# Hybrid decoder step: the compressed-branch bias read back through DRAM, position weights as the streamed operand, one source for the norms' mean, and constant products on TensorE inside three norms

## The chip, the cores and the metric

The kernel runs on one core of one Trainium2 chip. The metric is the device time of one execution in microseconds. The engines are TensorE (PE, its weight load PEld), VectorE (DVE), ScalarE (ACT), GpSimd (POOL) and SyncE (SP); SP issues DMAs and waits on semaphores.

## What is computed

One step of a two-layer decoder on 512 prompt tokens and 8 sequences of 8 new tokens, 576 tokens in all, 1024 features. Layer 1 is a Mamba-2 mixer, layer 2 an attention with three branches (compressed, selected, window) that read one shared K/V projection. Each layer has two normed residuals.

```python
def layer_norm(x, g, b):
    mu = jnp.mean(xf, axis=-1, keepdims=True)
    var = jnp.mean(jnp.square(xf - mu), axis=-1, keepdims=True)
    return ((xf - mu) * lax.rsqrt(var + LN_EPS)).astype(x.dtype) * g + b
# per layer
h = layer_norm(DN_ALPHA * h + mix, ln_g[i, 0], ln_b[i, 0])
h = layer_norm(DN_ALPHA * h + sq_relu_mlp(h, mlp_w1[i], mlp_w2[i]), ln_g[i, 1], ln_b[i, 1])
# compressed keys and values: 32 tokens each, a position row pe added to every token
part = chunks[:, r:r + n_cmp] + pe[r * CMP_STRIDE:(r + 1) * CMP_STRIDE][:, None, :]
hid = hid + jnp.einsum('bcjgd,jde->bcge', part, w1[r])
# compressed scores: a bias by distance, from a table of 32 buckets x 16 heads
s_c = s_c + bias_hgr[rel_bucket(pos[:, None] - cmp_end[None, :])].transpose(0, 2, 3, 1)
```

## The kernel before

**Layout and order.** Activations lie by feature: `xT` is 128 partitions x 8 chunks x 576 tokens. Every engine has its own program, written out by hand; semaphores order them, and each engine runs its program in order.

**Dense products.** Weights come as slots of 128 x 1024 (512 KB). SP loads a slot into one of two places of `ring`; ScalarE rounds it to the high part, GpSimd subtracts to the low part, into one of two places of `split`. A place of `ring` is free when its slot is split, a place of `split` when TensorE has used it. `dense_block` (line 1245) runs 48 products a slot: 8 chunks, three pairs of high and low parts, two halves of 288 tokens. `stream` on SP (line 594) is the loop of loads.

**Norms.** `last_projection` (line 1294) makes the projection ahead of a norm, eight blocks. VectorE adds each block to `xT` as it comes (`last_residuals`, line 1945) and adds chunks up into `row`: chunks 0 to 6 go into it, chunk 7 is left to TensorE as a second source. `layer_norm(k)` on TensorE (line 1486), for k = 0 to 3: sums by token of `row` (`by_token`: six products of 96 tokens x one column, two passes each) and of `xT`'s last chunk into `s1`, of the squares into `s2`; then the mean spread over all partitions into `flat_x`, from both sources (lines 1496, 1497); then, after VectorE and ScalarE have made 1/sqrt of the variance (lines 1968 to 1979), the scale spread into `flat_s` (line 1501). VectorE subtracts and multiplies by chunk (lines 1982, 1985), ScalarE applies g and b twice (lines 1106, 1107), once rounded into `xs`, and GpSimd makes the low part. The next projection's first block takes the chunks as they come.

**Bias tables.** Inside the first MLP, `bias_tables` on TensorE (line 1504) makes the bias by distance for 16 heads, `bt` (1040 distances), and then for the compressed branch `cbt`: 56 products of 128 distances x 16 heads (line 1517), one for each shift by 16. SP stores `bt` to DRAM (`bscr`, line 611), copies its rows 128 times to `bskew` (line 615), loads the strips `Rs` from there (line 619) and copies 16 pieces of them into `nr` (line 624), with one pair of weight slots in between each time. These stand in SP's program among the loads for the second matrix of the first MLP half, `S_M2[0][0]`.

**Compression weights.** `cw1` (2 MB) holds the compression's first matrices. GpSimd issues its load (line 840) behind `mlp_los(0, 1, ...)`, that is behind the splits for the second norm's projection, since its place holds `ef`, `eb` and `bt` until then. The position rows times `cw1` are 32 products (`position_sums`, line 1540) with `cw1` held and one column streamed, five after each chunk of the K/V projection's first block; ScalarE copies the result to `hpe` (line 1110).

Of the kernel before, what the change touches and what calls it, by code (L numbers as in the profile page):

```python
# [85 lines left out]
def build(nc, a):  # L86

    with ExitStack() as ctx:
# [131 lines left out]
        at[0] = KC * T  # L220
        bd = carve(512)
# [54 lines left out]
        CEN, SQS = zip(*((v[:, 0, :], v[:, 1, :]) for v in (spare, spare_x, spare, spare_x)))  # L276
        ptab = sb("ptab", [1, NB * NPG], I32)
# [215 lines left out]
        s1 = dense[0:TQ, 0, 0:2 * TC].rearrange("p (c k) -> p c k", k=2)  # L493
# [96 lines left out]
        def _(sp):  # L590
# [3 lines left out]
            def stream(first, last):  # L594
                with sp.Fori(first // NSLOT, last // NSLOT) as i:
                    for j in range(NSLOT):
# [46 lines left out]
        def _(pool):  # L643
# [194 lines left out]
            pool.wait_ge(cbt_ready, 1)  # L838
# [78 lines left out]
        def _(act):  # L917
# [180 lines left out]
            def layer_norm(k):  # L1098

                act.wait_ge(ln_stats, 2 * k + 1)  # L1100
                act.activation(lnt[:, 2, :], lnt[:, 2, :], ACT.Sqrt, bias=eps[0:TQ, 0:1]).then_inc(ln_root, 1)
                for m in range(KC):
                    act.wait_ge(ln_scaled, k * KC + m + 1)
                    ends = dict(bias=lnb[:, k, m:m + 1], scale=lng[:, k, m:m + 1])
                    if k < 3:
                        act.activation(xs[:, 0, m, :], xT[:, m, :], ACT.Identity, **ends).then_inc(xh_ready, 1)
                    act.activation(xT[:, m, :], xT[:, m, :], ACT.Identity, **ends).then_inc(x_ready, 1)
                if k == 1:
                    act.wait_ge(pe_done, 1)
                    act.activation(hpe, dense[:, 3, 0:2], ACT.Copy).then_inc(hpe_ready, 1)  # L1110
# [133 lines left out]
        def _(pe):  # L1244
# [31 lines left out]
            def projection(b0, s0, blocks, nsl, hi, lo, ready=None, rounded=None, after=None):  # L1276

                for j in range(2):
                    dense_block(b0 + j, s0 + j * nsl, nsl, hi, lo, ready=ready if j == 0 else None,
                                rounded=rounded if j == 0 else None, after=after if j == 0 else None)  # L1280
                    if after and j == 0:
                        pe.wait_ge(hpe_ready, 1)
# [255 lines left out]
            pe.wait_ge(s_cw1, 16)  # L1538

            def position_sums(k):  # L1540


                for j in range(5 * k, min(5 * k + 5, 32)):
                    kv, i = divmod(j, 16)
                    mm = pe.matmul(dense[:, 3, kv:kv + 1], cw1[:, kv, i // 8, i % 8, :],
                                   cpe[:, kv, i // 8, i % 8:i % 8 + 1], start=i == 0, stop=i == 15)
                if k == KC - 2:
                    mm.then_inc(pe_done, 1)

            projection(B_KV, S_KV, SL_KV, 1, x_h, x_l, (x_split, 2 * KC), (xh_ready, KC), position_sums)
# [43 lines left out]
            def compressed(s_):  # L1596
                pe.wait_ge(hpe_ready, 1)
# [178 lines left out]
        def _(dve):  # L1776
# [168 lines left out]
            def last_residuals(k):  # L1945
# [13 lines left out]
                for m in range(2, KC):  # L1959
# [3 lines left out]
                    if m < KC - 1:  # L1963
                        dve.wait_ge(blk_evac, b0 + m + 1)
                        dve.wait_ge(ln_sum, 6 * k + m - 1)
                        dve.tensor_tensor(row[:, :], row[:, :], xT[:, m, :], ALU.add).then_inc(ln_sum, 1)

            def layer_norm(k):
                dve.wait_ge(ln_tok, 3 * k + 2)
                link(dve, "dve", dve.tensor_reduce(lnt[:, 0, :], s1, AX.X, ALU.add))  # L1970
                link(dve, "dve", dve.tensor_tensor(lnt[:, 1, :], lnt[:, 0, :], lnt[:, 0, :], ALU.mult))
                dve.wait_ge(ln_tok, 3 * k + 3)
                link(dve, "dve", dve.tensor_reduce(lnt[:, 0, :], s2, AX.X, ALU.add))
# [43 lines left out]
            flat = cbt.rearrange("p s h -> p (s h)")  # L2017
            dve.tensor_copy(flat[:, 0:512], bS[:, 0, :])
            dve.tensor_copy(flat[:, 512:NSIG * NH], bS[:, 1, 0:NSIG * NH - 512]).then_inc(cbt_ready, 1)
# [67 lines left out]
            def shift_compressed(qt):  # L2087
# [6 lines left out]
                dve.wait_ge(pcs_done, qt + 1)  # L2094
                s0 = 24 - 8 * qt
# [317 lines left out]
```

## Time and profile before

| | us |
|---|---|
| median of 3 runs | 2146.24 (2142.49 to 2151.03) |
| profiled execution, its own time | 2147.33 |
| its span | 2145.7 |
| granted TensorE clock, mean share of full | 0.937 |

The profile is one execution. Busy time is time in which an engine ran an instruction; a row of the timeline merges neighbours of one form and says what ended the idle time ahead of them. Windows give the granted clock of TensorE as a share: 1.00 is 2.4 GHz, 0.50 is 1.2 GHz. Products in fp32 run as two passes, each counted as an instruction. DMA issues on SP stand as SPq rows.

### The profile page before, as it was taken

The page shows a single profiled execution, that of the slowest core. Times are in us where ns is not written, and L with a number is a line of the kernel's source. Part 1 is how long each engine was busy: PE and PEld are TensorE (multiplying, and loading weights), DVE is VectorE, ACT ScalarE, POOL GpSimd, SP SyncE. Part 2 cuts the span into 40 slices and gives each one's busy share as a digit, 9 for nine tenths or more (in the row PEclk, how much of TensorE's full clock was granted, in tenths as well). Part 3 has the DMA queues.
Part 4 walks back from the last instruction along what each step waited for, and adds up shares of the span by engine and source line. Part 5 has one row for each costly group of instructions (what it writes and reads, how often), then busy time and mean ns, then how long its engine had stood idle before and what let it go on. Part 6 is the DMA issues. An engine that isn't in the chain of part 4 may idle for free.

```text
span 2145.7 us, 36763 instructions
## 1 busy us (share of the span) xinstructions
PE 1982.5 (92%) x14824; PEld 1817.4 (85%) x14824; DVE 866.9 (40%) x1712; ACT 652.0 (30%) x1115; POOL 973.5 (45%) x697
## 2 busy tenths in 40 slices
PE   7989898978979998999999998989978999999997
PEld 5988887857778998999998998955547899999996
DVE  7484766847455210012233112167745621002134
ACT  3443343432133211122223113166634422112222
POOL 2444445446437642356453333344412565345552
PEclk9999999978998988999996998989999899999998
DMA  4211213122131215322221243350060122222221
GB/s 167 71 50 64 104 40 119 50 81 92 50 114 60 81 67 127 100 79 80 87 79 69 79 152 116 87 204 1 21 236 25 56 79 86 81 79 88 79 79 64
DMA packets 52629, 184.61 MB, mean 86 GB/s; under 512 B 7070, under 2 KB 11838, under 8 KB 50976
## 3 DMA queue, kind: packets, MB, share of 16 engines
q1 hardware_dynamic: 40272, 129.66, 18.3%
q0 software_dynamic: 9952, 50.08, 6.5%
q10 hardware_dynamic: 2288, 3.23, 0.4%
q8 instruction: 84, 1.38, 0.3%
q14 instruction: 33, 0.27, 0.0%
HBM read 166.59 MB, written 27.28 MB: 90 GB/s over the span
## 4 chain that ended last, share of the span: by engine, by line
PE 68%; DVE 12%; issue 9%; POOL 5%; ACT 4%; DMA 1%; ACTq 0%; SPq 0%; POOLq 0%; DVEq 0%
PE dense L1269 48%; PE dense L1592 3%; POOL split L673 3%; DVE tile L1908 2%; PE dense L1675 2%; PE bS L1381 2%; DVE tile L1818 2%; PE dense L1632 1%; PE bXM L1662 1%; POOL tile L780 1%; POOL hid L805 1%; PE bXM L1443 1%; PE bXM L1388 1%; PE dense L1710 1%; DVE tile L1811 1%
## 5 line engine op out<-in xcount | busy, mean ns | idle before, releaser
L1269 PE MATMUL dense<-xs,split 128*128 128x288 f32 x6848 | 984.7, 302 | 32.3 <-DVE y_lo L1936 9.2
L1269 PEld LDWEIGHTS dense<-xs,split 128*128 128x128 f32 x6848 | 948.7, 193 | 64.5 <-issue 51.7
L673 POOL TENSOR_TENSOR split<-ring,split 128x1024 fp32r<-128x1024 f32 x212 | 533.6, 2517 | 846.6 <-ACT split L932 825.4
L932 ACT ACTIVATE split<-ring 128x1024 fp32r<-128x1024 f32 x212 | 224.6, 1059 | 830.5 <-PE dense L1269 816.1
L1269 PE MATMUL dense<-hid,split 128*128 128x288 f32 x3072 | 417.1, 298 | 6.0 <-POOL split L673 6.0
L1269 PEld LDWEIGHTS dense<-hid,split 128*128 128x128 f32 x3072 | 415.6, 191 | 6.3 <-POOL split L673 6.3
L1830 DVE SCALAR_TENSOR_TENSOR tile<-tile,dense 128x576 f32<-128x576 f32 (+1 forms) x56 | 42.2, 754 | 422.9 <-PE dense L1269 422.9
L1995 DVE TENSOR_SCALAR sq<-dense 128x576 f32<-128x576 f32 x64 | 48.5, 758 | 310.5 <-PE dense L1269 310.5
L903 POOL TENSOR_SCALAR tile<-tile,tile,tile 128x128 f32<-128x128 f32 (+3 forms) x128 | 78.3, 626 | 80.1 <-DVE tile L2159 80.1
L805 POOL TENSOR_TENSOR hid<-sq,hid 128x576 f32 x64 | 77.2, 1206 | 0.0
L1171 ACT ACTIVATE tile<-tile,tile 128x128 f32<-128x128 f32 (+3 forms) x128 | 70.5, 553 | 18.2 <-DVE tile L2144 18.0
L1818 DVE SCALAR_TENSOR_TENSOR tile<-tile,tile,tile 128x512 f32<-128x512 f32 x72 | 69.5, 966 | 2.6
L1592 PE MATMUL dense<-tile,tile 128*128 128x128 f32 x576 | 66.4, 274 | 0.8 <-issue 0.8
L1592 PEld LDWEIGHTS dense<-tile,tile 128*128 128x128 f32 x576 | 64.9, 188 | 1.9 <-issue 1.2
L1960 DVE SCALAR_TENSOR_TENSOR tile<-tile,tile 128x576 f32<-128x576 f32 x24 | 61.8, 2575 | 0.0
L1118 ACT ACTIVATE hid<-sq 128x576 f32 x64 | 44.0, 687 | 44.3 <-DVE sq L1998 44.3
L1269 PE MATMUL dense<-y_lo,split 128*128 128x288 f32 x256 | 56.1, 301 | 0.0
L1908 DVE SCALAR_TENSOR_TENSOR tile<-tile,tile,tile 128x128 f32<-128x128 f32 (+1 forms) x80 | 53.8, 734 | 0.7
L1632 PE MATMUL dense<-tile,tile 64*128 64x128 f32 (+3 forms) x128 | 47.8, 491 | 6.2 <-DVE tile L2136 4.6
L1675 PE MATMUL dense<-tile,tile 128*64 128x256 f32 x384 | 51.8, 391 | 0.0
L1998 DVE TENSOR_TENSOR sq<-sq 128x576 f32<-128x576 f32 x64 | 48.5, 758 | 2.2
L1632 PE MATMUL bS<-tile,tile 64*128 64x128 f32 (+3 forms) x128 | 48.9, 495 | 0.4 <-DVE tile L2099 0.4
(316 smaller groups left out, 2174.0 us busy)
## 6 DMA issues: line engine op xcount, KB each, us to landing
ring<-in_w SPq DMA_DIRECT2D x212, 512.0 KB, 3.3
tile<-in_state POOLq DMA_DIRECT2D x4, 2048.0 KB, 9.4
o_sssm<-tile POOLq DMA_DIRECT2D x4, 2048.0 KB, 7.5
tile<-in_cmp POOLq DMA_DIRECT2D x32, 256.0 KB, 3.3
tile<-in_win POOLq DMA_DIRECT2D x8, 1024.0 KB, 6.0
tile<-in_sel SPq DMA_DIRECT2D x32, 256.0 KB, 5.1
o_kv<-tile POOLq DMA_DIRECT2D x1, 3456.0 KB, 14.1
bskew<-bscr SPq DMA_DIRECT2D x1, 3072.0 KB, 22.6
```

The costliest lines, as they stand in the source:

```text
L673: pool.tensor_tensor(split[:, j, 1, :], ring[:, j, :], split[:, j, 0, :].bitcast(F32), ALU.subtract).then_inc(w_split, 1)
L805: pool.tensor_tensor(hid[:, 1, m, :], sq[:, j, :], hid[:, 0, m, :].bitcast(F32), ALU.subtract).then_inc(hid_ready, 1)
L903: last = pool.tensor_scalar(pb(u, r)[:, 0:n], pb(u, r)[:, 0:n], wt[:, u % 2, r:r + 1], gate, ALU.mult, ALU.mult)
L932: act.activation(split[:, j, 0, :], ring[:, j, :], ACT.Copy).then_inc(w_hi, 1)
L1171: last = act.activation(pb(u, r)[:, 0:n], pb(u, r)[:, 0:n], ACT.Exp, bias=nmx[:, u % 4, r:r + 1], accum_out=sm[:, u % 4, r:r + 1])
L1269: mm = pe.matmul(dense[:, 2 * par + h_, 0:HT], split[:, j, w, cols], v[:, kk, h_ * HT:(h_ + 1) * HT], start=kk == 0 and t == 0, stop=kk == ...
L1592: mm = pe.matmul(dense[:, 2 * (s_ % 2) + kv, r * P:(r + 1) * P], cw1[:, kv, r, j, :], rows, start=j == 0, stop=j == 7)
L1632: pe.matmul(SB[k][:, 0:(qt + 1) * P], qT[half_of(h_), gp * GR + r, tok(qt)], kvT[half_of(h_), 4 * (br + 1) + gp, 0:(qt + 1) * P], start=Tr ...
L1675: mm = pe.matmul(OBANK[half_of(g), rr * 2 * P:(rr + 1) * 2 * P], v, PT[t % 4][:, h_ * 2 * P:(h_ + 1) * 2 * P], start=br == 0 and kt == 0, ...
L1818: dve.scalar_tensor_tensor(o[:, 0:NP_TOK], r[:, k:k + NP_TOK], cw[:, x, k:k + 1], o[:, 0:NP_TOK], ALU.mult, ALU.add)
L1908: last = dve.scalar_tensor_tensor(yt[:, j * L:(j + 1) * L], xg[:, j, tok(c)], dsk[:, g * 4 + j:g * 4 + j + 1], yt[:, j * L:(j + 1) * L], A ...
L1960: link(dve, "dve", dve.scalar_tensor_tensor(xT[:, m, :], xT[:, m, :], alpha, CEN[k], ALU.mult, ALU.subtract))
```

## The change

Compressed bias: `bias_tables` makes 8 products instead of 56, each of 128 distances x 16 heads. VectorE copies them to `btT`; SP stores `btT` to `bscr` (by distance, 16 heads a row) and loads `cbt` from there with 56 DMAs of 128 rows x 64 bytes, each from another first distance. VectorE's compressed scores wait for them. Norms: VectorE adds chunk 7 to `row` as well; TensorE takes sums and mean from `row` alone, squares first. `fill` puts products on TensorE at three places of a norm: in norms 1, 3 and 4 (k = 0, 2, 3) products of two constants whose result nobody reads, in norm 2 (k = 1) the 32 position products, now with a column of `cpe` held and `cw1` streamed into one row; that row is turned into columns by two small products after the first K/V block. The load of `cw1` itself stays where it was in GpSimd's program; the wait ahead of it names `cbt_done` in place of `cbt_ready`.

```diff
@@ SP
+            sp.wait_ge(bt_ready, 2)
+            sp.dma_start(bass.AP(a["bscr"].tensor, 0, [[NH, P], [NH * P, 8], [1, NH]]), btT).then_inc(bt_stored, 16)
             stream(s_bias + 2 * NSLOT, s_bias + 3 * NSLOT)
+            sp.wait_ge(bt_stored, 32)
+            for i in range(NSIG):
+                sp.dma_start(cbt[:, i, :], bass.AP(a["bscr"].tensor, (X0 + CB0 - CS * i) * NH, [[NH, P], [1, NH]])
+                             ).then_inc(cbt_ready, 16)
             sp.wait_ge(strips_loaded, 16)
             for h in range(NH):
                 sp.dma_start(nr[h * NS:(h + 1) * NS, :], Rs[0:NS, h, 0:P + 2 * NS]).then_inc(rows_loaded, 16)
@@ GpSimd
-            pool.wait_ge(cbt_ready, 1)
+            pool.wait_ge(cbt_done, 1)
             pool.wait_ge(bt_stored, 16)
             pool.dma_start(cw1, a["cw1"]).then_inc(s_cw1, 16)
@@ ScalarE, layer_norm(1)
                     act.wait_ge(pe_done, 1)
+                    act.activation(posr[0:1, :], dense[0:1, 2, 0:2 * P], ACT.Copy).then_inc(hpe_ready, 1)
+                    act.wait_ge(pe_done, 2)
                     act.activation(hpe, dense[:, 3, 0:2], ACT.Copy).then_inc(hpe_ready, 1)
@@ TensorE, after the first K/V block
+                    if b0 == B_KV and j == 0:
+                        position_columns()
+                        pe.wait_ge(hpe_ready, 2)
@@ TensorE
+            def position_sums(first, last):
+                for j in range(first, last):
+                    kv, i = divmod(j, 16)
+                    mm = pe.matmul(dense[0:1, 2, kv * P:(kv + 1) * P], cpe[:, kv, i // 8, i % 8:i % 8 + 1],
+                                   cw1[:, kv, i // 8, i % 8, :], start=i == 0, stop=i == 15)
+                if last == 32:
+                    mm.then_inc(pe_done, 1)
+            def position_columns():
+                pe.wait_ge(hpe_ready, 1)
+                for kv in range(2):
+                    mm = pe.matmul(dense[:, 3, kv:kv + 1], posr[0:1, kv * P:(kv + 1) * P], ones[0:1, 0:1],
+                                   start=True, stop=True)
+                mm.then_inc(pe_done, 1)
+            def fill(k, place):
+                if k == 1:
+                    if place == 0:
+                        pe.wait_ge(s_cw1, 16)
+                    position_sums(*((0, 3), (3, 16), (16, 32))[place])
+                else:
+                    for _ in range((2, 3, 4 if k < 3 else 0)[place]):
+                        pe.matmul(dense[:, 3, 0:2 * P], ident[:, :], triu[:, :, :], start=True, stop=True)
             def layer_norm(k):
                 b0 = ENDS[k][0]
-                pe.wait_ge(ln_sum, 6 * (k + 1))
-                by_token(s1, 0, row)
                 pe.wait_ge(blk_evac, b0 + KC)
-                by_token(s1, 1, xT[:, KC - 1, :]).then_inc(ln_tok, 1)
+                fill(k, 0)
                 pe.wait_ge(ln_sq, (k + 1) * KC)
                 by_token(s2, 1, sq[:, 1, :]).then_inc(ln_tok, 1)
+                pe.wait_ge(ln_sum, 7 * (k + 1))
+                by_token(s1, 0, row).then_inc(ln_tok, 1)
                 for cols in (slice(0, 512), slice(512, T)):
-                    pe.matmul(flat_x[:, cols], onesd[:, :], row[:, cols], start=True, stop=False)
-                    mm = pe.matmul(flat_x[:, cols], onesd[:, :], xT[:, KC - 1, cols], start=False, stop=True)
+                    mm = pe.matmul(flat_x[:, cols], onesd[:, :], row[:, cols], start=True, stop=True)
                 mm.then_inc(ln_wide, 1)
+                fill(k, 1)
                 pe.wait_ge(ln_stats, 2 * k + 2)
                 for cols in (slice(0, 512), slice(512, T)):
                     mm = pe.matmul(flat_s[:, cols], ones[0:TQ, :], SQS[k][0:TQ, cols], start=True, stop=True)
                 mm.then_inc(ln_wide, 1)
+                fill(k, 2)
@@ TensorE, bias_tables
-                for i in range(NSIG):
-                    o_ = i * NH
-                    x0 = X0 + CB0 - CS * i
-                    mm = pe.matmul(bS[:, o_ // 512, o_ % 512:o_ % 512 + NH], ef[:, x0:x0 + P], relb[:, :],
+                for i in range(8):
+                    mm = pe.matmul(bS[:, 0, i * NH:(i + 1) * NH], ef[:, i * P:(i + 1) * P], relb[:, :],
                                    start=True, stop=True)
@@ TensorE, ahead of and in the K/V projection
-            pe.wait_ge(s_cw1, 16)
-            def position_sums(k):
-                for j in range(5 * k, min(5 * k + 5, 32)):
-                    kv, i = divmod(j, 16)
-                    mm = pe.matmul(dense[:, 3, kv:kv + 1], cw1[:, kv, i // 8, i % 8, :],
-                                   cpe[:, kv, i // 8, i % 8:i % 8 + 1], start=i == 0, stop=i == 15)
@@ VectorE
-                    if m < KC - 1:
-                        dve.wait_ge(blk_evac, b0 + m + 1)
-                        dve.wait_ge(ln_sum, 6 * k + m - 1)
-                        dve.tensor_tensor(row[:, :], row[:, :], xT[:, m, :], ALU.add).then_inc(ln_sum, 1)
+                    dve.wait_ge(blk_evac, b0 + m + 1)
+                    dve.wait_ge(ln_sum, 7 * k + m - 1)
+                    dve.tensor_tensor(row[:, :], row[:, :], xT[:, m, :], ALU.add).then_inc(ln_sum, 1)
@@ VectorE, bias tables
-            dve.tensor_copy(flat[:, 0:512], bS[:, 0, :])
-            dve.tensor_copy(flat[:, 512:NSIG * NH], bS[:, 1, 0:NSIG * NH - 512]).then_inc(cbt_ready, 1)
+            dve.tensor_copy(btT.rearrange("p s h -> p (s h)"), bS[:, 0, 0:8 * NH]).then_inc(bt_ready, 1)
@@ VectorE, compressed scores
+                dve.wait_ge(cbt_ready, 16 * NSIG)
...
```

## Rows read from the trace of the kernel before

**Rows 1.** The page, part 1: busy time, share of the span, instructions.
```profile
PE 1982.5 (92%) x14824; PEld 1817.4 (85%) x14824; DVE 866.9 (40%) x1712; ACT 652.0 (30%) x1115; POOL 973.5 (45%) x697
```

**Rows 2.** Timeline of TensorE at the bias tables: start, length, line, operation, count, idle before.
```profile
787.01 23.10 PE L1517 MATMUL bS<-tile,tile 128*128 128x16 f32 x112 [1.45 <-DVE tile L2015]
809.95 12.30 PE L1269 MATMUL dense<-hid,split 128*128 128x288 f32 x72
```

**Rows 3.** Timeline of SP's DMA issues behind the bias tables.
```profile
835.44 6.73 SPq L599 DMA_DIRECT2D ring<-in_w  x2
852.21 0.39 SPq L619 DMA_DIRECT2D tile<-bskew  x1
857.04 2.65 SPq L599 DMA_DIRECT2D ring<-in_w  x2
860.93 10.86 SPq L624 DMA_DIRECT2D tile<-tile  x16
872.15 43.27 SPq L599 DMA_DIRECT2D ring<-in_w  x8
```

**Rows 4.** Timeline of the other engines in the same stretch.
```profile
853.54 1.06 ACT L932 ACTIVATE split<-ring 128x1024 fp32r<-128x1024 f32 x1 [14.19 <-DMA ring<-in_w]
...
857.07 43.09 PE L1269 MATMUL dense<-hid,split 128*128 128x288 f32 x300 [6.02 <-POOL split L673]
...
873.11 0.76 DVE L1830 SCALAR_TENSOR_TENSOR tile<-tile,dense 128x576 f32 x1 [21.14 <-PE dense L1269]
...
885.92 0.76 DVE L1830 SCALAR_TENSOR_TENSOR tile<-tile,dense 128x576 f32 x1 [12.06 <-PE dense L1269]
```

**Rows 5.** SP's lines by source, 780 to 900 us: ns min/median/max; landing in us.
```profile
L599 SPq DMA_DIRECT2D ring<-in_w x13: 327/333/1899, 781.4 to 895.9; - x13
...
DMA to landing us min/median/max: 3.1/3.4/18.0
...
L624 SPq DMA_DIRECT2D tile<-tile x16: 624/624/805, 860.9 to 871.2; - x16
```

**Rows 6.** Timeline of the first norm, k = 0.
```profile
662.69 1.10 PE L1290 MATMUL dense<-onesd,row 128*96 128x1 f32 x12
662.96 0.75 DVE L1830 SCALAR_TENSOR_TENSOR tile<-tile,dense 128x576 f32<-128x576 f32 x1 [3.53 <-PE dense L1269]
...
664.81 1.69 PE L1290 MATMUL dense<-onesd,sq 128*96 128x1 f32 x12
...
666.35 2.06 PE L1496 MATMUL bXM<-row,onesd 128*128 128x512 f32 x2
...
670.65 1.95 PE L1501 MATMUL bS<-tile,ones 96*128 96x512 f32 x4
...
672.71 0.75 DVE L1985 TENSOR_TENSOR tile<-tile,bS 128x576 f32<-128x576 f32 x1 [1.05 <-PE bS L1501]
...
687.66 0.76 DVE L1995 TENSOR_SCALAR sq<-dense 128x576 f32<-128x576 f32 x1 [4.02 <-PE dense L1269]
```

**Rows 7.** The chain that ended last: passes of 128 columns in fp32, start, length.
```profile
1329.51 7.34 PE dense L1592 x64
```

**Rows 8.** Windows, TensorE: length, busy (instructions), granted clock, DMA share, GB/s.
```profile
665.20:668.60 3.40, 3.40 (x12) 0.50 0.02 5
...
1143.10:1173.80 30.70, 28.12 (x124) 0.50 0.04 15
```

**Rows 9.** Timeline from the second norm's last residual to the K/V projection's first product.
```profile
1131.33 0.76 DVE L1830 SCALAR_TENSOR_TENSOR tile<-tile,dense 128x576 f32<-128x576 f32 x1 [9.44 <-PE dense L1269]
...
1136.11 0.56 POOL L840 DMA_DIRECT2D tile<-in_cw  x1
...
1145.67 1.81 PE L1269 MATMUL dense<-xs,split 128*128 128x288 f32 x6 [4.73 <-DMA tile<-in_cw]
```

**Rows 10.** Timeline of VectorE at the K/V projection's first two blocks.
```profile
1171.38 0.76 DVE L2029 TENSOR_SCALAR tile<-dense 128x576 f32 x1 [19.39 <-PE dense L1269]
1179.02 0.76 DVE L2029 TENSOR_SCALAR tile<-dense 128x576 f32 x1 [6.88 <-PE dense L1269]
```

More of the change, by code:

```diff
@@ L220, in build @@
         at[0] = KC * T
+        btT = carve(8, NH)
+        at[0] = KC * T
         bd = carve(512)
@@ L276, in build @@
         CEN, SQS = zip(*((v[:, 0, :], v[:, 1, :]) for v in (spare, spare_x, spare, spare_x)))
+        posr = row[0:1, 0:2 * P]
         ptab = sb("ptab", [1, NB * NPG], I32)
@@ L492, in build @@
         flat_s = bS.rearrange("p a b -> p (a b)")[:, 0:T]
-        s1 = dense[0:TQ, 0, 0:2 * TC].rearrange("p (c k) -> p c k", k=2)
+        s1 = dense[0:TQ, 0, 0:TC].unsqueeze(2)
         s2 = dense[0:TQ, 1, 0:2 * TC].rearrange("p (c k) -> p c k", k=2)
@@ L1274, in dense_block, with projection @@
                     mm.then_inc(w_used, 1)
-            def projection(b0, s0, blocks, nsl, hi, lo, ready=None, rounded=None, after=None):
+            def projection(b0, s0, blocks, nsl, hi, lo, ready=None, rounded=None):
                 for j in range(2):
                     dense_block(b0 + j, s0 + j * nsl, nsl, hi, lo, ready=ready if j == 0 else None,
-                                rounded=rounded if j == 0 else None, after=after if j == 0 else None)
-                    if after and j == 0:
-                        pe.wait_ge(hpe_ready, 1)
+                                rounded=rounded if j == 0 else None)
+                    if b0 == B_KV and j == 0:
+                        position_columns()
+                        pe.wait_ge(hpe_ready, 2)
                 with pe.Fori(1, blocks // 2) as i:
@@ L1536, in _ @@
             layer_norm(1)
-            pe.wait_ge(s_cw1, 16)
-            def position_sums(k):
-                for j in range(5 * k, min(5 * k + 5, 32)):
-                    kv, i = divmod(j, 16)
-                    mm = pe.matmul(dense[:, 3, kv:kv + 1], cw1[:, kv, i // 8, i % 8, :],
-                                   cpe[:, kv, i // 8, i % 8:i % 8 + 1], start=i == 0, stop=i == 15)
-                if k == KC - 2:
-                    mm.then_inc(pe_done, 1)
-            projection(B_KV, S_KV, SL_KV, 1, x_h, x_l, (x_split, 2 * KC), (xh_ready, KC), position_sums)
+            projection(B_KV, S_KV, SL_KV, 1, x_h, x_l, (x_split, 2 * KC), (xh_ready, KC))
             projection(B_Q, S_Q, SL_Q, 1, x_h, x_l)
@@ L1596, in compressed @@
             def compressed(s_):
-                pe.wait_ge(hpe_ready, 1)
+                pe.wait_ge(hpe_ready, 2)
                 if s_:
@@ L1962, in last_residuals @@
                     residual(b0 + m, m, 1.0, s0 + (m + 1) * nsl)
-                    if m < KC - 1:
-                        dve.wait_ge(blk_evac, b0 + m + 1)
-                        dve.wait_ge(ln_sum, 6 * k + m - 1)
-                        dve.tensor_tensor(row[:, :], row[:, :], xT[:, m, :], ALU.add).then_inc(ln_sum, 1)
+                    dve.wait_ge(blk_evac, b0 + m + 1)
+                    dve.wait_ge(ln_sum, 7 * k + m - 1)
+                    dve.tensor_tensor(row[:, :], row[:, :], xT[:, m, :], ALU.add).then_inc(ln_sum, 1)
             def layer_norm(k):
                 dve.wait_ge(ln_tok, 3 * k + 2)
-                link(dve, "dve", dve.tensor_reduce(lnt[:, 0, :], s1, AX.X, ALU.add))
-                link(dve, "dve", dve.tensor_tensor(lnt[:, 1, :], lnt[:, 0, :], lnt[:, 0, :], ALU.mult))
+                dve.tensor_reduce(lnt[:, 0, :], s2, AX.X, ALU.add)
                 dve.wait_ge(ln_tok, 3 * k + 3)
-                link(dve, "dve", dve.tensor_reduce(lnt[:, 0, :], s2, AX.X, ALU.add))
+                link(dve, "dve", dve.tensor_copy(lnt[:, 1, :], s1[:, :, 0]))
+                link(dve, "dve", dve.tensor_tensor(lnt[:, 1, :], lnt[:, 1, :], lnt[:, 1, :], ALU.mult))
                 dve.tensor_tensor(lnt[:, 2, :], lnt[:, 0, :], lnt[:, 1, :], ALU.subtract).then_inc(ln_stats, 1)
```

1 line of the change is left out of this document (removed).

## The prediction

> **What bounds the kernel now.** I read the page's busy shares first: TensorE is busy 92% of the span [rows 1], so the question for each edit is whether it takes products off TensorE or makes TensorE wait. Then, by the timeline, the four places that the diff touches: the bias tables inside the first MLP, SP's queue behind them, the norms, and the first block of the K/V projection.
>
> At the bias tables TensorE runs 112 passes (56 products, two passes each) from 787.01 to 809.95 and goes straight on with the next projection [rows 2]: nothing else is late there, so a pass less is time less.
>
> Behind it SP serves two things in one queue: the weight slots, and the bias copies through DRAM. [rows 3] show the walk: a weight slot at 835.44, the strips at 852.21, two slots at 857.04, sixteen row copies from 860.93, and the next slot only at 872.15. [rows 4] show what a late slot costs: the slot issued at 835.44 landed late, ScalarE's half of its split waited 14.19 us for that DMA, and TensorE stood still for 6.02 us until 857.07. The block of two slots after that stall ended 873.11 - 857.07 = 16.0 us later, the next took 885.92 - 873.11 = 12.8 us: a restart costs 3.2 us besides the stall. So the weight stream has little slack, and it is what an inserted queue of DMAs hits.
>
> In a norm, [rows 6]: the last residual ends at 663.71 (662.96 + 0.75), the first scaled chunk starts at 672.71, and the first MLP block is taken at 687.66, that is 14.95 us after that chunk, paced by ScalarE and GpSimd and not by TensorE (its 48 products need 6.4 us, half of the 12.8 above). So a norm is worth what moves 672.71.
>
> In the second norm, [rows 9]: the residual ends at 1132.08, GpSimd issues the load of cw1 at 1136.11, and the projection's first product waits for it until 1145.67. That block ends at 1171.38 and the next at 1179.02, 7.64 us later [rows 10].
>
> **Compressed bias, TensorE's share.** 56 products become 8. One pass costs (809.95 - 787.01) / 112 = 0.205 us [rows 2]; 16 passes cost 3.3 us. Saved: 22.9 - 3.3 = **19.7 us**, all on the path. The copy out of PSUM on VectorE gets smaller and TensorE's next products don't wait for it.
>
> **Compressed bias, SP's share.** Added are one store of btT, a wait for it, and 56 loads of 8 KB, and they stand ahead of the 16 row copies and of the weight slot that was issued at 872.15. Nothing shows these loads in the trace, so I bound one issue by its neighbours on SP: 0.333 us for a weight slot, 0.389 for the strips [rows 3, 5], both with 128 partitions out of DRAM like the new ones, against a row copy: 10.86 / 16 = 0.68 us from one to the next, with 8 partitions inside SBUF [rows 3, 5]. I take 0.38 (a slot and the gap behind it), nearest in shape; ends 0.335 and 0.68. 56 x 0.38 = 21.3 us.
>
> The walk in the old kernel's times: strips landed 860.93; the store of btT is queued behind them, 1 us (0 to 4); 21.3 us of issues; the row copies, 872.15 - 860.93 = 11.2; so the slot is issued at 894.4. It lands 3.4 us later [rows 5] (the median of the loop's loads is near the least there) and is split and used 857.07 - 853.54 = 3.5 us after that [rows 4]: 901.3. TensorE wants it at 885.9. Stall 15.4 us, with the restart of 3.2: **+18.6 us** (16.1 to 38.4). In general the stall is 56 x pitch - 5.9. The whole walk moves 19.7 us earlier with the tables, products and queue alike, so the difference stands. Behind it the ring fills within a slot or two. The waits added on SP queue only what is named here; VectorE's new wait for the 56 loads comes at the attention, hundreds of us later, and costs nothing.
>
> The Trainium skill (DMA: Bandwidth & Descriptors, section Rules for kernel authors) says to coalesce small transfers, under 64 KB paying mostly overhead; its fixed cost of 2 us, fitted on the GpSimd path, would make 112 us of 56 in a row. The row copies follow each other at 0.68 us, so the latencies overlap here and only the issue is paid.
>
> **Norms 1, 3 and 4.** Now: 9.0 us from residual to first chunk. After: fill, squares by token, sums by token, mean, then the longer of fill and statistics, then the scale. With TensorE at 2.4 GHz: two fills are 4 passes of 256 columns at 0.23 (a 128-column pass is 7.34 / 64 = 0.115 us [rows 7]), 0.9; two groups by token at 1.10 each [rows 6], 2.2; mean 1.1 (half of the four half-rate pieces between 666.35 and 670.65, 4.3, is 2.2 at the lower clock) and three fills 1.4, which cover the statistics; scale 1.3. Sum 6.9: -2.1 us. With TensorE at 1.2 GHz: 1.8 + 2 x 1.69 + 2.2 + 2.8 + 2.0 [rows 6] = 12.2: +3.2 us. Today the granted clock is 0.50 in the mean while TensorE is busy all of it [rows 8], after groups of one-column products. The change puts wide products around two such groups, but the groups still follow each other for 2.2 us. I take the middle of a clock that falls in some of them: **0**, bounds -6.3 and +9.6 for three. The last fill (4 products, 1.8 us) lies under the first chunk's 1.7 us on VectorE and ScalarE and under the paced block behind it; without that cover it costs its 1.8.
>
> The Trainium skill (TensorE: Matmul & The Clock Gate, part on HAM oscillation) lays a fall to gaps in which TensorE waits. Row and rule differ: here it fell while TensorE was busy 3.40 of 3.40 us [rows 8]. By the rule alone the fills, which close the gaps, would hold the clock and give the -6.3.
>
> **Norm 2 and the K/V block.** The 32 position products leave the K/V block and become the fills of this norm: 3, 13 and 16. The edit streams cw1's 128 columns and holds one column, so a product costs two passes of 0.115 to 0.23. But the first fill waits for cw1, and the load is issued where it was: behind GpSimd's last split for the projection ahead of this norm. So the wait that held the projection until 1145.67 [rows 9] now holds the whole norm. From there: 3 products 0.7 to 1.4; two groups by token 2.2 to 3.4; mean 1.1 to 2.2; 13 products 3.0 to 6.0; scale 1.3 to 2.0. 8.3 to 15.0; I take 12, since TensorE comes out of a 13.5 us wait and so starts at the lower clock. First chunk at 1157.7, block end 14.95 later: 1172.6. The last 16 products (3.7 to 7.4 us) and the block's 6.4 fit under the 14.95. Then the row is turned into columns, with two hand-offs to ScalarE, some 1 us: 1173.6 against 1171.38. The old block ran at 0.50 throughout [rows 8] and so did part of the next, 7.64 instead of 6.4 [rows 10]; that 1.2 comes back. **+1.0 us** (-2.7 to +4.0). The gain that the edit reaches for, a block without its 32 one-column products, is used up by the wait.
>
> **Sum.** -19.7 + 18.6 + 0 + 1.0 = -0.1 us. The profiled execution took 2147.33, so 2147.2 by it; the median of the runs is 1.1 lower, and I give 2146 on its scale. A measurement of this kernel can tell about 0.5%, 10.7 us, from no change.
>
> **Rivals.**
> - *Slower: the loads go out like the row copies.* At 0.68 us each SP is held 38.1 us, the stall is 32.2, and the sum +16.7: 2163. It speaks for it that those are SP's only long series of small DMAs; against, that the shape (128 partitions) is the slots'. From 0.57 us a load on, the result is over 0.5% slower.
> - *Faster: the clock holds.* All four norms at their low bound (-6.3, and -3.7 below my +1.0), issues at 0.335 (-2.5): -12.6, 2133. For it: the fills stand where TensorE waits. Against: the 2.2 us of one-column products in a row.
> - *Faster: the queue is hidden.* No stall: -18.7, 2127. That would need 56 issues in 5.9 us, 0.1 us each, and no slot took under 0.327 [rows 5].
> - *The fills don't do what they say:* clock low throughout the three norms, +9.6: 2155.
>
> **How the numbers follow.** Forecast 0.53 (2146, own range 2137 to 2155); clock low 0.12; slow issues 0.20; clock holds 0.12; queue hidden 0.03. The clock cases end near the 0.5% line, so: faster 0.15, same 0.63, slower 0.22. The range reaches into both outer cases: 2134 to 2163.
>
> **What would show it.** SP: 56 loads from one to the next at 0.38, the slot behind them issued some 22 us later against the products than now. TensorE: an idle stretch of 15 us in the first MLP, before the first product of the sixth block of that half, released by GpSimd's split; the bias products 3.3 us. Second norm: TensorE idle some 13 us right after the residual, released by the load of cw1. Norms: granted clock in the mean, and 9 us from residual to first chunk give or take 2. I am wrong if TensorE doesn't wait in that MLP, if the load of cw1 has landed before the second norm, or if the fills delay the scale by more than 3 us a norm.

## The result and the profile after

| | before, us | changed, us | changed / before |
|---|---|---|---|
| first comparison, medians | 2146.8 (2142.49 to 2151.13) | 2160.41 (2153.16 to 2164.0) | 1.0057 [1.0039, 1.0075] |
| second comparison, medians | 2149.81 | 2156.86 (2145.06 to 2160.12) | 1.0026 [1.0007, 1.0044] |
| profiled execution, its own time | 2147.33 | 2158.77 | |
| its span | 2145.7 | 2157.1 | |
| granted TensorE clock, mean share of full | 0.937 | 0.942 | |

The changed kernel is slower, in the first comparison by more than the 0.5% that a measurement can tell from no change, in the second by about half of that; both intervals lie above 1. The second comparison is that of the run `e11_changed_again`, which also left a second trace of the changed kernel ("changed again" below).

I cut the span at events that all kernels have: the end of the last residual ahead of each norm, VectorE's first take of the block behind it, its eighth residual in the first MLP's second matrix, and its take of the second K/V block.

| stretch, us | before | changed | changed again |
|---|---|---|---|
| start to the residual of norm 1 | 663.71 | 660.25 | 666.90 |
| norm 1, to the first MLP block | 23.95 | 25.09 | 25.07 |
| first half of the MLP (tables, SP's queue) | 236.66 | 239.41 | 240.02 |
| rest of the MLP, to the residual of norm 2 | 207.76 | 207.76 | 207.76 |
| norm 2, to the first K/V block | 39.29 | 40.94 | 42.45 |
| second K/V block | 7.64 | 7.49 | 7.52 |
| attention, to the residual of norm 3 | 512.35 | 516.61 | 514.63 |
| norm 3, to the next MLP block | 24.02 | 26.50 | 23.46 |
| second MLP, to the residual of norm 4 | 406.30 | 406.30 | 406.30 |
| norm 4, to the end | 23.98 | 26.74 | 23.45 |

The rows that the change touches (norms, first half, K/V) came out 10.6 us longer in the first trace and 6.4 in the second. The two rows that it leaves alone, the start and the attention, moved by -3.5 and +4.3, and by +3.2 and +2.3. Over the 14 traces of this case (before, changed and the runs below) the start, whose code is the same in all of them, took from 659.6 to 671.9 us, and the attention, the same but for the loads and reads of the compressed bias's table, from 510.3 to 519.9. Both go with TensorE's granted clock there: the longest start has the lowest mean of the fourteen (0.92), the shortest the highest (0.94), and so in the attention (0.93 and 0.96). One trace can't price an edit by its span, and I read each edit in its own stretch.

**Tables** [rows 2], timeline of TensorE in the changed kernel: start, length, line, operation, count, idle time before it.

```profile
784.69 2.63 PE L1558 MATMUL bS<-tile,tile 128*128 128x16 f32 x16 [1.45 <-DVE tile L2041]
787.16 3.23 PE L1281 MATMUL dense<-hid,split 128*128 128x288 f32 x12
```

From the first product to the next projection 787.16 - 784.69 = 2.5 us, where [rows 2] had 22.9.

**SP's queue** [rows 3], timeline of SP's issues in the changed kernel, and by source the 56 loads (ns min/median/max; landing).

```profile
829.37 0.39 SPq L623 DMA_DIRECT2D tile<-bskew  x1
829.81 2.52 SPq L626 DMA_DIRECT2D bscr<-tile  x1
834.21 2.68 SPq L603 DMA_DIRECT2D ring<-in_w  x2
838.95 26.78 SPq L630 DMA_DIRECT2D tile<-bscr  x56
865.77 10.85 SPq L634 DMA_DIRECT2D tile<-tile  x16
876.99 32.47 SPq L603 DMA_DIRECT2D ring<-in_w  x7
```

```profile
L630 SPq DMA_DIRECT2D tile<-bscr x56: 319/432/494, 838.9 to 865.3; - x56
DMA to landing us min/median/max: 1.6/1.7/1.9
```

The store's issue takes 2.52 us. The loads wait for it to land, until 838.95, and hold SP for 26.78 us: 26.78 / 56 = 0.478 us from one to the next, though the shortest issue among them took 0.319, a slot's price. The second load went out 0.37 us after the first; from there on 0.474 from one to the next is the rule. Each lands 1.7 us after its issue, so the landings don't pile up: the issuing looks like the price, which the runs below test. The slot behind goes out at 876.99. What that does [rows 4], timeline of the other engines:

```profile
863.09 0.76 DVE L1857 SCALAR_TENSOR_TENSOR tile<-tile,dense 128x576 f32 x1 [12.06 <-PE dense L1281]
880.43 1.06 ACT L942 ACTIVATE split<-ring 128x1024 fp32r<-128x1024 f32 x1 [29.21 <-DMA ring<-in_w]
883.97 31.30 PE L1281 MATMUL dense<-hid,split 128*128 128x288 f32 x218 [21.04 <-POOL split L683]
899.14 0.75 DVE L1857 SCALAR_TENSOR_TENSOR tile<-tile,dense 128x576 f32 x1 [35.30 <-PE dense L1281]
911.95 0.75 DVE L1857 SCALAR_TENSOR_TENSOR tile<-tile,dense 128x576 f32 x1 [12.06 <-PE dense L1281]
```

The split on ScalarE waited 29.21 us for that slot, TensorE 21.04 us for the split. The block after the stall took 899.14 - 883.97 = 15.2 us, the next 911.95 - 899.14 = 12.8; from one residual to the next it is 899.14 - 863.09 = 36.05 over the stall.

**Norm 1** [rows 6], timeline of the changed kernel (PE: TensorE, DVE: VectorE), and three windows of it (length, busy with instructions, granted clock, DMA share, GB/s) [rows 8].

```profile
659.50 0.75 DVE L1857 SCALAR_TENSOR_TENSOR tile<-tile,dense 128x576 f32<-128x576 f32 x1 [3.53 <-PE dense L1281]
660.30 1.13 PE L1527 MATMUL dense<-triu,ident 128*128 128x256 f32 x4 [0.92 <-DVE tile L1857]
661.27 1.10 PE L1303 MATMUL dense<-onesd,sq 128*96 128x1 f32 x12
662.24 1.49 PE L1303 MATMUL dense<-onesd,row 128*96 128x1 f32 x12
663.58 2.37 PE L1538 MATMUL bXM<-row,onesd 128*128 128x512 f32 x4
665.14 0.76 DVE L2003 TENSOR_TENSOR tile<-ident,lnt 96x576 f32<-96x576 f32 x1
665.75 2.87 PE L1527 MATMUL dense<-triu,ident 128*128 128x256 f32 x6
668.42 1.84 PE L1543 MATMUL bS<-tile,ones 96*128 96x512 f32 x4
670.37 0.76 DVE L2011 TENSOR_TENSOR tile<-tile,bS 128x576 f32<-128x576 f32 x1 [3.62 <-PE bS L1543]
```

```profile
658.00:660.48 2.48, 1.56 (x13) 1.00 0.09 36
660.48:662.96 2.48, 2.48 (x25) 0.99 0.00 0
662.96:665.44 2.48, 2.48 (x9) 0.50 0.03 7
```

The residual ends at 660.25, the first scaled chunk starts at 670.37: 10.12 us against 9.0. L1527 are the constant products, L1543 the scale. VectorE had the scale's operand ready at 665.14 + 0.76 = 665.90, yet the scale went out at 668.42, behind the constant products of 665.75. The clock is at 1.00 up to the one-column products (L1303), and at 0.50 from 662.96 on, with TensorE busy 2.48 of 2.48 us.

**Norm 3**, timeline and window of the changed kernel; the residual ends at 1697.56.

```profile
1697.61 2.07 PE L1527 MATMUL dense<-triu,ident 128*128 128x256 f32 x4 [0.92 <-DVE tile L1857]
1699.48 1.97 PE L1303 MATMUL dense<-onesd,sq 128*96 128x1 f32 x12
```

```profile
1697.20:1699.60 2.40, 1.99 (x6) 0.50 0.00 0
```

Here the clock is down before the first constant product, which takes its place ahead of the products by token: four passes take 2.07 us where norm 1 took 1.13. Norm 3 took 11.47 us, norm 4, where the clock fell 0.3 us behind the residual, 11.72.

**Norm 2** [rows 9, 10], timeline of the changed kernel.

```profile
1131.76 0.75 DVE L1857 SCALAR_TENSOR_TENSOR tile<-tile,dense 128x576 f32<-128x576 f32 x1 [9.45 <-PE dense L1281]
1136.54 0.56 POOL L850 DMA_DIRECT2D tile<-in_cw  x1
1146.12 1.44 PE L1504 MATMUL dense<-tile,tile 128*1 128x128 f32 x6 [14.47 <-DMA tile<-in_cw]
1153.65 3.37 PE L1504 MATMUL dense<-tile,tile 128*1 128x128 f32 x26
1156.95 1.30 PE L1543 MATMUL bS<-tile,ones 96*128 96x512 f32 x4
1158.36 0.75 DVE L2011 TENSOR_TENSOR tile<-tile,bS 128x576 f32<-128x576 f32 x1 [3.84 <-PE bS L1543]
1173.22 0.60 PE L1513 MATMUL dense<-ones,row 1*128 1x1 f32 x4
1173.46 0.76 DVE L2053 TENSOR_SCALAR tile<-dense 128x576 f32 x1 [4.17 <-PE dense L1281]
1174.09 11.08 PE L1281 MATMUL dense<-xs,split 128*128 128x288 f32 x81 [0.26 <-ACT tile L1122]
```

TensorE stands idle for 14.47 us right behind the residual, for the load of `cw1`. From its first position product to the first chunk it takes 12.24 us, and the block is taken 15.10 us after that.

### The profile page after: what moved, and what is told of

It reads as the page before. It is cut to its first block and busy times, and to the rows that moved or that the text cites. A ratio compares the mean times of both kernels' runs of the same rounds, so it can differ in the third digit from the quotient of the medians.

```text
span 2157.1 us, 36604 instructions
## 1 busy us (share of the span) xinstructions
PE 1958.2 (91%) x14714; PEld 1790.7 (83%) x14714; DVE 864.8 (40%) x1715; ACT 652.8 (30%) x1116; POOL 972.8 (45%) x697
## 5 line engine op out<-in xcount | busy, mean ns | idle before, releaser
L1281 PE MATMUL dense<-xs,split 128*128 128x288 f32 x6848 | 979.1, 301 | 30.3 <-POOL xs L804 10.6
```

The source lines that it names most:

```text
L1281: mm = pe.matmul(dense[:, 2 * par + h_, 0:HT], split[:, j, w, cols], v[:, kk, h_ * HT:(h_ + 1) * HT], start=kk == 0 and t == 0, stop=kk == ...
```

## The experiments

Where the 56 loads stand in SP's queue, what they are made of, and the constant products were tried first one at a time. Each run gives its median, the ratio to the kernel before beside it, and a 95% interval; a norm's time is that from the last residual to the first scaled chunk.

**The loads late.** SP's 56 loads and the wait ahead of them move behind the loop that streams the first MLP's and the K/V projection's weights.

```diff
             stream(s_bias + 2 * NSLOT, s_bias + 3 * NSLOT)
-            sp.wait_ge(bt_stored, 32)
-            for i in range(NSIG):
-                sp.dma_start(cbt[:, i, :], ...).then_inc(cbt_ready, 16)
...
             stream(s_bias + 3 * NSLOT, S_O + 2 * NSLOT)
+            sp.wait_ge(bt_stored, 32)
+            for i in range(NSIG):
+                sp.dma_start(cbt[:, i, :], ...).then_inc(cbt_ready, 16)
```

> The changed kernel with one thing moved: SP's wait for the store of btT and the 56 loads of cbt stand behind the loop that streams the weight slots up to the attention's output projection, where SP only waits for the attention. Theory (queue): in the first MLP TensorE stands 21.0 us for the slot that SP issues behind the 56 loads, and the block after it takes 2.4 us longer; both vanish, so the time falls by some 23 us against the changed kernel, to about 2137, and the idle stretch at the sixth block is gone. Rival (transfer): the store and the loads themselves, wherever they stand, disturb the weight stream, or another wait takes the stall's place there; then TensorE still stands over 10 us in that stretch and the time falls by less than 12 us.

2133.84 us, ratio 0.9938 [0.9911, 0.9964]. TensorE has no wait over 6 us left in that MLP, and its first half takes 214.63 us instead of 239.41: -24.8. The loads now go out at 1279 to 1308 us; TensorE's longest wait from 1275 to 1320 us is one of some 4 us for VectorE, as in the changed kernel. The block with the stall is 36.05 - 12.8 = 23.2 us shorter, and that is the queue's price; the other 1.5 us lie between the bias products and the block behind them, which scatters that much from trace to trace.

**The tables alone, loads late.** The kernel before with the eight products, the store and the late loads, its norms untouched.

> The kernel before with the compressed bias of the change alone (8 products, btT, its store, 56 loads), and the loads moved behind the weight stream as in the first of these runs; norms and position products are those of the kernel before. Theory (queue): the saved products, 20.5 us in the trace of the changed kernel, stay saved: 19 to 21 us below the kernel before, about 2126. Rival (transfer or cover): TensorE was to stand in that MLP for another reason, the bias rows' copy through DRAM, and part of the products lay in its shade: less than 12 us below the kernel before.

2128.39 us, ratio 0.9922 [0.9898, 0.9946]: 2149.0 - 2128.39 = 20.6 us less, the price of the 96 passes. Its norms 1, 3 and 4 took 9.00, 8.98 and 8.97 us, as before. The run above differs from it by the edits of the norms and position products alone and is 5.4 us longer, with intervals that overlap: the times don't show a price of these edits.

**One load instead of 56,** in the place of the 56. The table is then read in the reverse order of the shifts.

```diff
-            for i in range(NSIG):
-                sp.dma_start(cbt[:, i, :], bass.AP(a["bscr"].tensor, (X0 + CB0 - CS * i) * NH, [[NH, P], [1, NH]])
-                             ).then_inc(cbt_ready, 16)
+            sp.dma_start(cbt, bass.AP(a["bscr"].tensor, (X0 + CB0 - CS * (NSIG - 1)) * NH, [[NH, P], [CS * NH, NSIG], [1, NH]])
+                         ).then_inc(cbt_ready, 16)
```

> The changed kernel with the 56 loads of cbt made one DMA of 128 x 56 x 64 bytes at the same place in SP's queue (the shifts then lie in rising order and are read backwards). Theory (issue): what starves the weight slots is SP's time to issue, 0.475 us from one load to the next; with one issue the slot behind it goes out about 26 us earlier, the 21 us wait of TensorE at the sixth block is gone or under 3 us, and the time falls by 19 to 24 us against the changed kernel. Rival (pieces): what matters are the 7168 pieces of 64 bytes on the DMA engines, which the slots queue behind; then the wait stays over 8 us and the time falls by less than 13 us.

2136.27 us, ratio 0.9937 [0.9911, 0.9964]; the first half took 214.59 us, without the stall. SP's issues in this kernel:

```profile
837.94 0.38 SPq L629 DMA_DIRECT2D tile<-bscr  x1
838.36 14.13 SPq L633 DMA_DIRECT2D tile<-tile  x16
852.87 31.12 SPq L603 DMA_DIRECT2D ring<-in_w  x7
```

The same 7168 pieces of 64 bytes go out in one issue of 0.38 us and land 6.0 us later. The row copies behind it take 14.13 us instead of 10.85, one of them 4.10 to issue, and the slot still goes out at 852.87. So it is the number of issues on SP that costs; the small pieces by themselves hold SP some 3.3 us there, without a stall.

**No constant products:** the counts (2, 3, 4) in `fill` become 0 in norms 1, 3 and 4; their result isn't read.

> The changed kernel without the constant products in norms 1, 3 and 4 (the order of the sums, the single source and the position products in norm 2 stay). Theory (they lie on the path at the lower clock): in the changed kernel the granted clock falls in these norms all the same, and the products then take 0.44 us each between the sums and the scale; without them the stretch from the last residual to the first scaled chunk falls from 10.1 to 11.7 us to 7.5 to 9 us in each of the three, and the time by 4 to 9 us. Rival (they hold the clock): without them TensorE runs more of the norm and of the block behind it at 1.2 GHz; the stretch stays or grows, the time is the same or up to 5 us longer.

2153.84 us, ratio 1.0023 [1.0007, 1.004]. The three norms took 8.20, 8.65 and 8.66 us, within the theory's 7.5 to 9. In the first the clock falls 2.6 us behind the residual, as with the constants: they don't hold it there.

**cw1 early.** The load and the two waits ahead of it move on GpSimd ahead of the last shares of the second norm's splits.

```diff
+                    if k == 0:
+                        pool.wait_ge(cbt_done, 1)
+                        pool.wait_ge(bt_stored, 16)
+                        pool.dma_start(cw1, a["cw1"]).then_inc(s_cw1, 16)
...
-            pool.wait_ge(cbt_done, 1)
-            pool.wait_ge(bt_stored, 16)
-            pool.dma_start(cw1, a["cw1"]).then_inc(s_cw1, 16)
```

> The changed kernel with GpSimd's issue of the load of cw1 moved ahead of its splits for the projection before norm 2 (same waits ahead of it). Theory (arrival): the norm waits for the load from 1132.5 to 1146.1, 13.6 us, and nothing else is late; with the load landed the first K/V block ends about 27 us after the last residual in place of 40.9, and the time falls by 11 to 15 us. Rival (products): the 13 position products ahead of the scale and the hand-offs behind the block are what cost; then the stretch from residual to first scaled chunk stays above 18 us and the time falls by less than 6 us.

2138.6 us, ratio 0.9956 [0.993, 0.9983]. From the residual of norm 2 to the first K/V block 25.16 us instead of 40.94, -15.8: 14.47 of these are the wait. The time fell by more than the 11 to 15 us expected.

**Wide products between the one-column ones.** Ahead of each one-column product of the two groups by token in norms 1, 3 and 4 stands a constant product of 128 columns.

```diff
+                    if between:
+                        pe.matmul(dense[:, 3, 0:P], ident[:, :], triu[:, 0, :], start=True, stop=True)
```

> The changed kernel with a constant product of 128 columns ahead of each of the 12 one-column products in the two groups by token, in norms 1, 3 and 4. Theory (the groups by token bring the clock down): with wide products among them the granted clock stays 1.00 from the last residual to the scale in all three norms; the stretch from residual to first scaled chunk is then the same in all three, about 6.8 (the changed kernel's best) plus 12 x 0.23 = 9.6 us, where the changed kernel showed 10.1, 11.5 and 11.7 in one execution and 6.8 to 10.1 in others. Rival (the clock falls for another reason, the idle gap ahead of the fill or the block before): it still falls in some of them, and those take 12 us or more.

2166.43 us, one execution. The first norm in five windows, and its mean and scale:

```profile
671.90:673.84 1.94, 1.90 (x13) 1.00 0.00 0
673.84:675.78 1.94, 1.94 (x21) 1.00 0.03 8
675.78:677.72 1.94, 1.94 (x21) 1.00 0.25 44
677.72:679.66 1.94, 1.94 (x12) 1.00 0.57 226
679.66:681.60 1.94, 1.94 (x10) 1.00 0.44 115
```

```profile
677.83 1.27 PE L1540 MATMUL bXM<-row,onesd 128*128 128x512 f32 x4
680.29 1.19 PE L1545 MATMUL bS<-tile,ones 96*128 96x512 f32 x4
```

The clock stays at 1.00 through the whole norm, and so it did in norm 3. The mean takes 1.27 us instead of 2.37, the scale 1.19 instead of 1.84. But each group by token now takes 2.5 us or more where it took 1.1 to 1.5, and both norms 9.71 us, where norms of the changed kernel's form in which the clock stayed up took 6.76 to 7.10. In norm 4 the clock fell 0.4 us behind the residual, ahead of any product by token, and the norm took 11.36. So the theory held in two norms of three; that the products between held the clock there isn't shown, since it also stayed up in 3 of 18 norms without them.

**Which constant products cost.** Without the three between mean and scale, and with these three alone:

> The three constant products between mean and scale are left out; those ahead of the squares and behind the scale stay. Theory A: they stand in the path wherever the clock is low, since the diagonal on VectorE is ready within 0.2 us of the mean's end and the scale then waits for them; in the first norm of the changed kernel the scale went out at 668.42 though the diagonal was ready at 665.90. Then residual to first chunk falls to 8.2 to 9.0 us in norms 1, 3 and 4 (10.1 to 11.7 in the changed kernel), and the time to 2150 to 2157. Rival B: they hold TensorE's clock up for the scale, which took 1.84 us with them and 2.39 without any; then the norms stay at 10 to 12 us and the time at 2158 to 2164.

> The reverse: only the three constant products between mean and scale are kept. Theory A: the norms stay at 10 to 11.7 us where the clock is low, and at 6.7 to 7.2 where it isn't; time 2156 to 2162. Rival B (the price lies with the other two places, these three help): 8.0 to 8.6 us in all three norms, time 2150 to 2154.

2154.55 us, 1.0031 [1.0013, 1.0048], and 2159.74 us, 1.0035 [1.001, 1.0059]; the changed kernel beside them 2156.86. The times don't tell them apart, the norms do: 8.20, 8.20 and 7.30 us against 9.95, 10.00 and 9.94. Norm 1 without the three:

```profile
663.34 2.38 PE L1538 MATMUL bXM<-row,onesd 128*128 128x512 f32 x4
664.86 0.75 DVE L2003 TENSOR_TENSOR tile<-ident,lnt 96x576 f32<-96x576 f32 x1
665.67 2.39 PE L1543 MATMUL bS<-tile,ones 96*128 96x512 f32 x4
668.17 0.75 DVE L2011 TENSOR_TENSOR tile<-tile,bS 128x576 f32<-128x576 f32 x1 [1.66 <-PE bS L1543]
```

The scale (665.67) now follows its operand (664.86 + 0.75 = 665.61) at once. It takes 2.39 us instead of 1.84, as rival B says, but it starts 2.5 us earlier against the operand. Theory A holds, and the clock's course is not what makes the difference: in norm 1 of the changed kernel it fell 2.6 us behind the residual, in norms 1 and 3 here 2.6 and 2.7, and the norms took 10.12, 8.20 and 8.20. So at the same fall the three products cost 1.9 us a norm. Without any constant product such a norm took 8.20 too (norm 1 of the run without them): the other two places cost it nothing.

**The changed kernel again.**

> The changed kernel once more, for a second trace of it and for times beside the other two. If the norms follow a fixed course of the clock, they take 10.1, 11.5 and 11.7 us again; if it is scatter, anything from 6.8 to 11.7, as in the kernels with one edit taken back (6.8 to 11.7 in nine norms). Time 2153 to 2164. TensorE's wait in the first MLP and the one in the second norm must come back within 0.5 us, since nothing in them depends on the clock.

2156.86 us. The norms took 10.12, 8.44 and 8.45 us: scatter, not a fixed course, though 10.1, 11.4 and 11.7 also stood in the kernel with one load and in the one with both moves, below. TensorE's wait in the MLP was 21.85 us (21.04), that for `cw1` 14.73 (14.47): 0.8 and 0.3 us off, the first more than I allowed.

**Towards a faster kernel.** Both moves together (loads late, `cw1` early):

> The changed kernel with both moves: the 56 loads behind the weight stream and the load of cw1 ahead of the splits before norm 2; the constant products stay. Theory (two separate waits): the two gains add up, some 23 to 26 and 14 to 16 us against the changed kernel: 2116 to 2124, about 1.3% below the kernel before. Rival (shared): the earlier load of cw1 takes the DMA engines from weight slots once nothing else holds TensorE, or a new wait comes in its place; then 2130 or more.

2119.96 us, 0.9862 [0.9826, 0.9897]; norms at 10.12, 11.47 and 11.72. The gains add up as expected. Then no constant products at all, and the 32 position products with their wait all behind the scale of norm 2:

> As the one before, without the constant products, and with all 32 position products behind the scale of norm 2, under the first chunks (the wait for cw1 there too). Theory: against the one before, norms 1, 3 and 4 take 8.2 to 8.7 us from residual to first chunk in every execution in place of 6.8 to 11.7, 0.5 to 1 us less each on the mean, and norm 2 loses the 13 products ahead of its scale, 1.5 us: 2112 to 2120, 1 to 5 us below it. Rival (the constants pay on the mean): it is the same or up to 4 us slower than the one before.

2110.12 us (2104.97 to 2119.02), 0.9834 [0.979, 0.9878], an interval that overlaps that of the run before it; norm 4, at 9.32, lies above the 8.7 expected. In the traces the three norms gained 7.1 us against the run before it and norm 2 another 2.2 (26.78 to 24.54). Then with the constant products in the two harmless places:

> The kernel with both moves (the 56 loads late, cw1 early with all 32 position products behind the scale), now with the constant products ahead of the squares and behind the scale, and none behind the mean. If what the run without those three showed carries over (norms 1, 3 and 4 at 8.2, 8.2 and 7.3 us against a mean of 8.6 without any constant product), the three norms take 7.3 to 8.2 us and the time is 1 to 3 us below the version without constants: 2106 to 2112, a ratio of 0.981 to 0.984. If the two places only shift where the clock comes back, the norms take 8.2 to 9.3 us as there, and the time is the same, 2108 to 2114. No wait over 10 us in the first MLP and none in the second norm in either case.

2115.12 us (2104.86 to 2117.32), 0.9826 [0.9793, 0.9858], norms at 8.19, 10.17 and 7.63. No gain from them; the 10.17 lies outside both expectations, and so does the median, though its ratio lies in the first. All three intervals lie below 1, and below those of the changed kernel.

The norms' times, where the constant products differ:

| constant products | norms seen | range, us | mean, us |
|---|---|---|---|
| kernel before (and its norms with the new tables) | 6 | 8.97 to 9.00 | 9.0 |
| all (changed kernel, again, and four with one or two moves) | 18 | 6.76 to 11.72 | 9.8 |
| none | 6 | 8.20 to 9.32 | 8.6 |
| ahead of the squares and behind the scale | 6 | 7.30 to 10.17 | 8.3 |
| between mean and scale alone | 3 | 9.94 to 10.00 | 10.0 |

What sets a norm's time apart within one row is when the clock falls, counted from the last residual (narrow windows of the traces give it). In the 18 norms with all constant products: not at all, 6.76 to 7.10 us (three norms); after 2.9 to 3.2 us and for a shorter while, 8.4 (three); after 2.6 to 2.7, 10.1 (six); between 0.5 ahead of it and 0.4 behind, 11.4 to 11.7 (six). In the six norms of the first row it fell after 0.95 to 1.52 us each time, and all took 9.0.

## Why the prediction went wrong

I forecast no change, from a sum of -0.1. By its terms, with the two traces of the changed kernel:

| term, us | forecast | measured | from |
|---|---|---|---|
| tables | -19.7 | -20.4, -20.6 | 22.9 - 2.5; the tables alone |
| SP's queue | +18.6 | +23.4 | 21.0 stall + 2.4 restart |
| norms 1, 3, 4 | 0 | +6.4 and 0.0 | stretches, first and second trace |
| norm 2 and K/V | +1.0 | +1.5 and +3.0 | stretches, first and second trace |
| sum | -0.1 | +10.9 and +6.0 | with -20.4 and +23.4 in both |

**The step that failed is the pitch of the loads:** "I take 0.38 (a slot and the gap behind it), nearest in shape". That held for the first load alone (0.37 to the second); a row of 56 goes out at 0.478, between the slot and the row copies (why the second load comes later than the first isn't shown). It made the queue cost 23.4 us instead of 18.6, more than the tables save. The rest of that step held: "the stall is 56 x pitch - 5.9" gives 20.9 with the measured pitch, and 21.04 was measured. The store was worth what I gave it: by source it landed 9.1 us after its issue, at 829.81 + 9.1 = 838.9, and the strips at 829.37 + 8.9 = 838.3. The restart cost 2.4 instead of 3.2. The rival of slow issues had the same mechanism at too high a price, 0.68. That its 2163 lies near the measured 2160 is chance: it stood on a queue of 35.4 us (32.2 and the restart), where 23.4 were measured and the norms and norm 2 brought another 7.9 in the first trace. Its point of decision (0.57 a load) assumed that the other terms stood.

**The second is the size of the norms.** Both ends came out: "6.9" was seen as 6.76 to 7.10 and "12.2" as 11.72. The upper one had luck in its parts: its 1.69 for a group by token is one in which the clock fell on the way; wholly at 0.50 a group took 1.97 to 2.06, and the scale, taken at 2.0, took 1.19 to 1.28 in norms 3 and 4, where the clock was back by then. "Three fills 1.4, which cover the statistics" holds at 1.00 but for 0.4 us (norm 4 with the loads late: operand ready at 2113.36, scale at 2113.75); at 0.50 they stand in the path, as the sum's 2.8 had it. What failed is the choice between the ends, "the middle of a clock that falls in some of them: 0": it fell in 15 of 18 norms, which lie 0.8 us above before in the mean, 2.5 us for three. That one trace gave +6.4 and the next 0.0 is the clock's scatter.

What brings the clock down stays open. The Trainium skill (TensorE: Matmul & The Clock Gate, part on HAM oscillation) lays such a fall to gaps in which TensorE waits. By that rule fills that leave no gap would hold the clock; it fell in 15 of 18 norms. The kernel before speaks against gaps alone: TensorE was busy 4.95 of the 5.20 us ahead of its fall in norm 1 (660.00 to 665.20). Where constant products open a norm they leave a gap of 0.92 us ahead of the first, and the clock fell in or behind it in most of these norms, not in all. The products by token of the norm itself are no general cause either: in norms 3 and 4 of the changed kernel the clock was down before the first of them.

**Norm 2** went as told: the wait for `cw1`, 12.24 us to the first chunk against the 12 that I took, the block 15.10 behind it, the hand-off 0.26. The 1.2 us that were to come back in the second K/V block didn't: 7.49 us against 7.64. The clock was back at 1.00 there, but the block's products started only at 1174.09, 0.63 us after the first block was taken, behind the hand-off that I had put ahead of that take.

**The tables** were right to 0.9 us, and the copy out of PSUM hid as told.

How the 7 to 14 us between the medians share out to the last few us stays open: the start and the attention scatter by 12 and 10 us, with the granted clock. What sets the clock there was not tried.

## What to carry to other kernels

A table that saves 20 us of products can cost more than that if it comes back by many small DMAs on the queue that feeds the weights: count the issues, take their pitch from a series and not from one, and put them behind the loads that TensorE is about to want, or fold them into one. A product that is to fill a wait belongs where it can't delay what ends the wait; check when the awaited operand is ready at the lower clock as well. Where the clock falls at another moment in every execution, compare stretches in which it fell alike. A load that gates a filler gates everything behind it on that engine.

## What the runs showed of the hardware

- 56 loads of 128 x 64 bytes from DRAM went out at 0.478 us each in a row (0.52 in the run with the loads late), the second 0.37 us after the first; each landed some 1.7 us later. As one DMA the same pieces took 0.38 us to issue and 6.0 to land.
- A store of 1024 pieces of 64 bytes held SP 2.52 us, where a slot of 512 KB holds it 0.33.
- TensorE's clock fell from 1.00 to 0.50 while it was busy: in norm 1 of the kernel before, behind 4.95 busy of 5.20 us that held groups of one-column products. With 128-column products between them it stayed at 1.00 in two norms and fell ahead of them in a third. Norm 4, with the same instructions, took 6.76, 8.45 or 11.72 us in three traces; in the fastest the clock never fell.
